# Two mean-removing norms: GpSimd adds one more tile, TensorE sums fewer groups, the mean is signalled earlier

## The reference

```python
def layer_norm(x, g, b, eps=1e-5):
    xf = x.astype(F32)
    mu = jnp.mean(xf, axis=-1, keepdims=True)
    xc = xf - mu
    var = jnp.mean(xc * xc, axis=-1, keepdims=True)
    return (xc * lax.rsqrt(var + eps) * g.astype(F32) + b.astype(F32)).astype(x.dtype)

# second_block, in each of its layers l = 0, 1
    sub = y @ w_out[l]
    x = layer_norm(ALPHA * x + (1.0 + gate[:, None, :]) * sub, ln_g[l], ln_b[l])
# x after l = 1 is the result
```

## Time and profile before

| | |
|---|---|
| median of 3 runs | 1328.61 us (1327.92 to 1329.54) |
| profiled execution | 1329.28 us, of which the span of instructions is 1327.4 us |
| granted TensorE clock, mean over the span | 0.995 |
| PE busy | 1291.9 us (97%) |
| DVE busy | 989.9 us (75%) |
| ACT busy | 670.6 us (51%) |
| POOL busy | 196.0 us (15%) |
| ln0, from the last projection product to the next layer's first | 1129.7 to 1138.2 us |
| ln1, from the last projection product to the end of the span | 1313.8 to 1327.4 us |

### The profile page before, as it was taken

One profiled execution on the slowest core, in us unless ns is written; L12 is line 12 of the kernel. 1 busy time (PEld: TensorE's weight loads), 2 busy tenths in 40 slices (PEclk: granted clock), 3 DMA queues, 4 the chain that ended last, 5 costly groups with the idle time before them and its releaser, 6 DMA issues. The chain is left out here.

```text
span 1327.4 us, 25032 instructions
## 1 busy us (share of the span) xinstructions
PE 1291.9 (97%) x9436; PEld 1146.1 (86%) x9436; DVE 989.9 (75%) x1734; ACT 670.6 (51%) x1358; POOL 196.0 (15%) x268
## 2 busy tenths in 40 slices
PE   7999999999999999999999999999999999999987
PEld 6786779888888888898896899999999988999967
DVE  5698778999887878979428666655666886865874
ACT  4427753631522524334237665566465566455573
POOL 0101223000000000123204610000220016120043
PEclk8999999999999999999999999999999999999999
DMA  7774124366895876944320146655485433455411
GB/s 293 300 212 149 54 81 159 132 225 219 321 309 206 298 255 245 313 140 148 114 90 17 57 156 208 200 192 188 143 278 179 140 123 110 162 174 177 167 49 48
DMA packets 67668, 233.20 MB, mean 176 GB/s; under 512 B 7280, under 2 KB 12400, under 8 KB 67312
## 3 DMA queue, kind: packets, MB, share of 16 engines
q1 hardware_dynamic: 67568, 231.84, 51.0%
HBM read 230.76 MB, written 1.05 MB: 175 GB/s over the span
## 5 line engine op out<-in xcount | busy, mean ns | idle before, releaser
L988 DVE TENSOR_TENSOR wlo<-raw,whi 128x1024 fp32r<-128x1024 f32 (+1 forms) x284 | 346.9, 1222 | 144.5 <-ACT whi L629 138.7
L629 ACT ACTIVATE whi<-raw 128x1024 fp32r<-128x1024 f32 (+1 forms) x284 | 296.6, 1045 | 257.2 <-PE ps L1743 254.5
L1741 PE MATMUL ps<-H,whi 128*128 128x256 f32 (+1 forms) x896 | 299.3, 334 | 3.1 <-DVE H L1121 0.9
L1742 PE MATMUL ps<-H,whi 128*128 128x256 f32 (+1 forms) x896 | 296.0, 330 | 0.0
L1743 PE MATMUL ps<-H,wlo 128*128 128x256 f32 (+1 forms) x896 | 295.8, 330 | 0.0
L1741 PEld LDWEIGHTS ps<-H,whi 128*128 128x128 f32 x896 | 168.7, 188 | 23.2 <-issue 4.4
L1743 PEld LDWEIGHTS ps<-H,wlo 128*128 128x128 f32 x896 | 168.8, 188 | 16.6
L1742 PEld LDWEIGHTS ps<-H,whi 128*128 128x128 f32 x896 | 169.0, 189 | 15.6
L1741 PE MATMUL ps<-Gh,whi 128*128 128x256 f32 x624 | 174.2, 279 | 0.5 <-DVE Gl L1195 0.4
L1741 PE MATMUL ps<-HID,whi 128*128 128x256 f32 (+1 forms) x536 | 174.5, 326 | 0.0
L1742 PE MATMUL ps<-HID,whi 128*128 128x256 f32 (+1 forms) x536 | 174.3, 325 | 0.0
(11 more groups left out here) (268 smaller groups left out, 2060.0 us busy)
## 6 DMA issues: line engine op xcount, KB each, us to landing
raw<-wall SPq DMA_DIRECT2D x270, 512.0 KB, 4.0
aring<-aall SPq DMA_DIRECT2D x144, 512.0 KB, 4.8
raw<-wall SPq DMA_DIRECT2D x14, 384.0 KB, 3.0
AL<-ali SPq DMA_DIRECT2D x14, 192.0 KB, 5.1
X<-xin SPq DMA_DIRECT2D x2, 1024.0 KB, 7.9
BI<-rpb SPq DMA_DIRECT2D x4, 512.0 KB, 10.0
out<-X SPq DMA_DIRECT2D x4, 256.0 KB, 2.5
cst<-const SPq DMA_DIRECT2D x1, 960.0 KB, 8.1
```

Source lines behind the costliest of these rows:

```text
L629: act.activation(whi[:, slot, b:b + n], raw[:, slot, 0:n], ACT.Copy).then_inc(sem("w_hi"), 1)
L988: dve.tensor_tensor(wlo[:, slot, b:b + n], raw[:, slot, 0:n], whi[:, slot, b:b + n].bitcast(F32), ALU.subtract)\
L1741: pe.matmul(o, a[0], b[0], start=first, stop=False)
L1742: pe.matmul(o, a[0], b[1], start=False, stop=False)
```

## The change

GpSimd's loop takes tile 6 and its square too. `moments` has six groups instead of nine: block and column of RS's sums first, then the block of tile 7, and behind it `mean_sum` is raised at once; then the column of tile 7, the column of RS's squares, and the column of tile 7's square. The wait for `tile_summed` now stands ahead of all of them. DVE centres three tiles ahead of `deviation` and four behind.

```diff
@@ DVE, end of a layer of the second block
                 dve.wait_ge(sem("mean_sum"), l + 1)
-                centre(0, 2)
+                centre(0, 3)
                 deviation(norms[f"ln{l}"])
-                link(centre(2, CENTRED))
+                link(centre(3, CENTRED))
@@ GpSimd
-                for k in range(1, KT - 2):
+                for k in range(1, KT - 1):
...
-                    pool.wait_ge(sem("tile_summed"), 5 * l + k)
+                    pool.wait_ge(sem("tile_summed"), 6 * l + k)
@@ TensorE, moments
-                pe.wait_ge(sem("out_added"), 23 + 8 * l)
-                pe.matmul(ps[:, 6, 0:N], ones, xt(KT - 2, N), start=True, stop=False)
-                part(4, xt(KT - 2, N), True, False)
-                pe.wait_ge(sem("sq"), n.t0 + n.n - 1)
-                part(0, SQ[:, (n.t0 + n.n - 2) % 4, 0:N], False, False)
-                pe.wait_ge(sem("tile_summed"), 5 * (l + 1))
-                pe.matmul(ps[:, 6, 0:N], ones, RS[:, 0:N], start=False, stop=False)
+                pe.wait_ge(sem("tile_summed"), 6 * (l + 1))
+                pe.matmul(ps[:, 6, 0:N], ones, RS[:, 0:N], start=True, stop=False)
+                part(4, RS[:, 0:N], True, False)
                 pe.wait_ge(sem("out_added"), 24 + 8 * l)
-                pe.matmul(ps[:, 6, 0:N], ones, xt(KT - 1, N), start=False, stop=True)
-                part(4, RS[:, 0:N], False, False)
-                part(4, xt(KT - 1, N), False, False).then_inc(sem("mean_sum"), 1)
+                pe.matmul(ps[:, 6, 0:N], ones, xt(KT - 1, N), start=False, stop=True).then_inc(sem("mean_sum"), 1)
+                part(4, xt(KT - 1, N), False, False)
+                pe.wait_ge(sem("sq_used"), n.t0 + n.n - 1)
+                part(0, RS[:, N:2 * N], False, False)
                 pe.wait_ge(sem("sq"), n.t0 + n.n)
-                part(0, SQ[:, (n.t0 + n.n - 1) % 4, 0:N], False, False)
-                pe.wait_ge(sem("sq_used"), n.t0 + n.n - 2)
-                part(0, RS[:, N:2 * N], False, True).then_inc(sem("sq_used"), 2)
+                part(0, SQ[:, (n.t0 + n.n - 1) % 4, 0:N], False, True).then_inc(sem("sq_used"), 1)
```

## The result

| | before | changed |
|---|---|---|
| median (16 runs each) | 1329.42 us (1327.27 to 1332.74) | 1332.53 us (1330.56 to 1333.91) |
| changed to before | | 1.0021, 95% interval 1.0015 to 1.0028 |
| profiled execution, span | 1327.4 us | 1329.9 us |
| granted clock, mean over the span | 0.995 | 0.993 |

A forecast was written before the change was run, and what follows sets the result against it. TensorE was held busy nearly throughout, waiting for GpSimd at ln0, its own groups setting ln1's end. ln0 +1.57 and ln1 -1.36 made +0.21 us: 1329.5 profiled, 1328.8 median, range 1327.7 to 1331.9.

The forecast's parts named there:

- ln0's sum: Layer 0's norm: later GpSimd sum and six groups cost +1.57 us, bounds +1.28 to +2.56.
- the first rival: At ln0 the clock falls to half while TensorE waits; total 1331.4 us, from 1329.8 to 1332.0; chance 0.38.
- the case in which the clock holds and the norms cancel: Main forecast: ln0 loses 1.57 us, ln1 gains 1.36, giving a median of 1328.8 us; chance 0.50.
- The wait and its place: At ln0 TensorE idles some 2.8 us, from about 1129.8 to 1132.68, waiting for GpSimd's sum of tile 6.
- The price of the fall: At ln0, 6.32 us at half clock, less 0.60 absorbed ahead of `spread`: 2.6 us, bounds 1.0 and 3.2.
- 0.13: At ln0, GpSimd's gap between the square of tile 5 and the sum of tile 6, taken as 0.13 us.
- 2.51: At ln0, the time from `deviation` to the scaling, set by `spread`, kept at 2.51 us as before.
- The uncontended 0.72 for the added sum: At ln0, GpSimd's sum of tile 6 takes 0.72 us as VectorE is idle; up to 0.99 more.
- the six groups' 2.86: In the norms, TensorE's six groups take 2.86 us from the first start to the last result.
- ln1: Layer 1's norm: GpSimd just in time, fewer groups gain 1.36 us; bounds about -0.4 and -1.6.

The follow-up runs named there:

- e3: The change made in layer 0's norm (ln0) alone, layer 1's as in the kernel before; ratio to before 1.0025 (1.0015 to 1.0035).
- e7: The changed kernel with three unread `keep` products ahead of TensorE's wait for GpSimd at ln0; ratio to before 1.0020 (1.0010 to 1.0029).
- e10: The changed kernel without its seven `keep` products at ln0; ratio to before 1.0024 (1.0015 to 1.0034).
- e8: e6 with two `keep` products added ahead of TensorE's wait in the sums of norms q0 and q1; ratio to before 0.9991 (0.9982 to 1.0000).
- e9: e5 with `keep` products added ahead of TensorE's waits, three at ln0, two each at q0 and q1; ratio to before 0.9997 (0.9988 to 1.0006).
- e1: The changed kernel with six unread `keep` products ahead of TensorE's wait for GpSimd at ln0; ratio to before 0.9998 (0.9987 to 1.0008).
- e2: The change made in layer 1's norm (ln1) alone, layer 0's as in the kernel before; ratio to before 0.9994 (0.9983 to 1.0005).
- e5: The changed kernel with GpSimd adding tile 6 ahead of the square of tile 5 at ln0; ratio to before 0.9997 (0.9988 to 1.0007).
- e6: ln1 as changed; ln0 with before's sums and groups, tile 7's block ahead of RS's, three tiles centred first; ratio to before 0.9993 (0.9984 to 1.0002).

## Why the prediction was wrong

*The step that failed* is ln0's sum, which had no term for the clock: it took full clock behind a wait of some 2.8 us, and the fall cost 2.39. The ground for leaving it out was the first rival's weighing. I put the fall at 0.38 and the case in which the clock holds and the norms cancel at 0.50, "against it, dense products stand right before the wait". The wait and its place were right, and the rival's price was nearly so; the argument against it was worth nothing. All four traces with a wait of 1.85 us or more (changed, e3, e7, e10) show the fall, e7 with `keep` products directly ahead of the wait.

The Trainium skill, "TensorE: Matmul & The Clock Gate", section "HAM oscillation — how this bites in real kernels", which I set beside the rival, tells of waits between bursts of products that put the clock back to half, so that the next burst begins cold. The traces agree in kind only: at ln0 the clock fell to 0.50 after 2.90 us without work, but the burst behind the wait began at 1.00 and ran so for some 1.7 us. And e8 fell while TensorE was busy throughout, e9 behind 0.42 us of idling, which that account does not cover.

*The price of the fall.* Predicted 2.6 us, within 1.0 to 3.2. Measured against e1, whose clock held: from the first group to `deviation` 3.76 us instead of 2.85 (+0.91), from there to the scaling 3.26 instead of 2.21 (+1.05, `keep` at half clock stands ahead of `spread`), and to the first product 2.12 instead of 1.69 (+0.43, the second `keep`). Together 2.39. The prediction's 2.6 came near it by another way: it took 6.32 us at half clock, less 0.60 that a gap absorbs; 6.8 us at half clock are 3.4 us of work not done, of which 1.0 did not reach the chain.

*ln0 without the fall.* Predicted +1.57. The changed kernel's 12.24 less 2.39 is 9.85, against 8.32: +1.53. That this is so near is luck: in it two errors cancel. GpSimd's tile 6 started 0.30 later than reckoned, after a gap of 0.42 us "issue" where I took 0.13; and the power after `deviation` started that much sooner (0.17 us behind VR, where the trace of before had 0.46), so that 2.51 became 2.21. Both are in all traces with the two added instructions in this order (e1, e3, e7, e10). The uncontended 0.72 for the added sum was right (0.72), and so were the six groups' 2.86 (2.81 in e1, 1131.68 to 1134.49).

*How late GpSimd is* varies with the execution: its sum of tile 6 ended 3.37 us behind the start of the last product in the changed kernel (1129.38 to 1132.75), 2.96 in e1 and 2.97 in e3. In the changed kernel, as in before, e2 and e7, GpSimd's square of tile 4 took 1.71 or 1.72 us beside VectorE's last subtraction of weights, which took 1.35 or 1.36; in the others that square took 0.73 or 0.74 and the subtraction 1.80 or 1.81. I had taken one execution's rows as fixed.

*ln1.* Predicted -1.36, measured -1.32 in the changed kernel and -1.53 in e1, e2 and others, where GpSimd was in time. `spread` now ends last, as forecast: the scaling waits 0.17 us for line 1843.

*The sum.* 1.57 + 2.6 - 1.36 = +2.8 us by the rival's terms; the ratio says 2.8 (2.0 to 3.7). The range ended at 1331.9, 0.6 below the median of 1332.53, and the baseline moved too: the kernel before has 1329.42 over 16 runs, 0.81 above the three that I had.

## What to carry to other kernels

Before products are taken off an engine that only waits with them, ask what the engine does instead: the tile 6 products looked spare at ln0, and yet they were work under a wait. Where the other engine is late, append nothing in front of what is waited for; with tile 6 moved ahead of a square that isn't needed yet (e5) the total stayed as before, and the same edit without that move cost 0.2%. Of the fillers tried, the one that covered all but 0.15 us of the wait held the clock (e1); those that left 1.85 and 0.42 did not in their traces (e7, e9). At half clock such products stand in the way themselves.

## What the runs showed of the hardware that I had not expected

The granted clock fell in e8 with TensorE busy throughout, for 3.4 us, on a stretch of which most products had 2 columns, while the same stretch in e6 kept 1.00. At q0 it fell in two of the twelve traces (e2, e3), at q1 in two (e1, e2), and not in the others. So a kernel near such a place has executions of either kind. Runs of one kernel lie 3 to 6 us apart (1327.27 to 1332.74 before), and those of before with the lower mean clock are the slower ones. What exactly tips the clock was not tried and stays open.

GpSimd's list has a gap of about 0.3 us: ahead of the power in the kernel before, ahead of tile 6's sum in the changed one ("0.42 <-issue"). It may belong to a place in the program, but e5 and e9, whose list has another order, show it at neither. Its cause is open.
